# Hybrid convolution and pooling decoder trunk: first gate block of each merge asked for inside the last input block, convolution taps handed out differently in the merge rounds

## The reference, cut to what matters

```python
# per layer, D_MODEL 2048, E = 1024; x (4, 2048, 2048), DEPTH 2
xn   = rms_norm(h, norm_g)
proj = xn @ w_in              # 9 slices of width E, then three gates of width 2048
a_in, a_b, a_c, a_z, b_in, b_z, c_val, c_gate, c_z, gates = split(proj)
y_a = a_b * causal_dwconv(a_c * a_in, 3 taps) * silu(a_z)
y_b = (pooled(b_in) @ pool_w) * pool_scale * silu(b_z)
v   = causal_dwconv(c_val * sigmoid(c_gate), 31 taps) + bias
y_c = silu(layer_norm(v)) * silu(c_z)
up      = [y_a @ w_bo[0], y_b @ w_bo[1], y_c @ w_bo[2]]       # E -> 2048 each
merged  = sum over b of sigmoid(gates[b]) * up[b]
h = h + merged @ w_o
h = h + sigmoid(h @ w_ple_gate) * (p @ w_ple_proj)
```

## Time and profile before

| | us |
|---|---|
| median of 3 runs | 2593.92 (2593.8 to 2594.42) |
| profiled execution | 2592.57 |
| its span, slowest core (core 1) | 2591.0 |
| spans of the eight cores | 2585.6 to 2591.0 |
| busy on core 1: TensorE, VectorE, ScalarE, GpSimd | 2512.6, 1560.5, 556.6, 119.4 |

### The profile page before, as it was taken

One profiled execution on the slowest core, in us unless ns is written; L12 is line 12 of the kernel. 1 busy time (PEld: TensorE's weight loads), 2 busy tenths in 40 slices (PEclk: granted clock), 3 DMA queues, 4 the chain that ended last, 5 costly groups with the idle time before them and its releaser, 6 DMA issues.

```text
span 2591.0 us, 35103 instructions; the slowest of 8 cores (2585.6 to 2591.0 us)
## 1 busy us (share of the span) xinstructions
PE 2512.6 (97%) x15468; PEld 1506.6 (58%) x15468; DVE 1560.5 (60%) x1534; ACT 556.6 (21%) x746; POOL 119.4 (5%) x217
## 2 busy tenths in 40 slices
PE   5999999999999999999999999999999999999997
PEld 2666667776667678766666655544554444444445
DVE  4567666865787753412447676777668885442156
ACT  6000002211212322112340000022112224221124
POOL 0000000000000000000000000000000000000001
PEclk9999999999999999999999999999999999999998
DMA  7434343444344444645553434334434444446453
GB/s 219 88 66 79 69 76 72 82 75 73 73 74 83 92 85 82 143 99 95 132 131 74 75 72 82 73 74 81 86 70 81 91 90 98 83 96 148 84 94 131
DMA packets 49848, 237.51 MB, mean 92 GB/s; under 512 B 4768, under 2 KB 18080, under 8 KB 26912
## 3 DMA queue, kind: packets, MB, share of 16 engines
q0 software_dynamic: 29056, 186.72, 40.1%
q1 hardware_dynamic: 20640, 48.54, 5.6%
HBM read 404.67 MB, written 17.29 MB: 163 GB/s over the span
## 4 chain that ended last, share of the span: by engine, by line
PE 89%; DVE 7%; ACT 1%; SPq 1%; issue 1%; DMA 1%; POOL 0%; DVEq 0%; ACTq 0%; POOLq 0%
PE psa L134 89%; DVE Tt L134 3%; DVE h L134 3%; SPq L134 1%; ACT Tt L134 1%; DVE yb L134 1%; DMA yb<-w_in 1%; DVE acc L134 0%; ACT L134 0%; POOL ring L134 0%; ACT psa L134 0%; ACT yb L134 0%; ACT acc L134 0%; DVEq L131 0%; DVEq L99 0%
## 5 line engine op out<-in xcount | busy, mean ns | idle before, releaser
L134 PE MATMUL psa<-xn,ring 128*128 128x352 bf16 (+8 forms) x8384 | 1365.4, 322 | 9.2 <-DVE Tt L134 5.3
L134 PEld LDWEIGHTS psa<-xn,ring 128*128 128x128 bf16 x8384 | 815.5, 97 | 541.6 <-DVE Tt L134 9.5
L134 DVE SCALAR_TENSOR_TENSOR h<-h,par_s 128x1056 f32<-128x1056 bf16 (+1 forms) x480 | 623.6, 1299 | 11.5
L134 DVE TENSOR_TENSOR Tt<-psa,Tt 128x1056 f32<-128x1056 f32 (+7 forms) x208 | 205.5, 989 | 517.1 <-PE psa L134 477.2
L134 ACT ACTIVATE Tt<-psa 128x512 f32<-128x512 f32 (+9 forms) x328 | 243.2, 742 | 1134.6 <-PE psa L134 1108.2
L134 PE MATMUL psa<-yb,ring 128*128 128x352 bf16 (+1 forms) x1920 | 343.5, 339 | 0.0
L134 PE MATMUL psa<-acc,ring 128*128 128x352 bf16 (+2 forms) x1664 | 292.7, 336 | 31.1 <-DVE acc L134 23.6
L134 PEld LDWEIGHTS psa<-yb,ring 128*128 128x128 bf16 x1920 | 186.5, 97 | 152.2
L134 PEld LDWEIGHTS psa<-acc,ring 128*128 128x128 bf16 x1664 | 161.9, 98 | 159.9 <-DVE acc L134 26.1
L134 DVE TENSOR_TENSOR Tt<-Tt 128x1056 f32<-128x1056 f32 (+9 forms) x130 | 136.0, 1046 | 121.3 <-ACT Tt L134 118.3
L134 PE MATMUL psa<-h 128*128 128x264 bf16 (+1 forms) x1152 | 185.1, 319 | 17.6 <-DVE h L134 16.0
(11 more groups left out here) (70 smaller groups left out, 928.9 us busy)
## 6 DMA issues: line engine op xcount, KB each, us to landing
ring<-w_in POOLq DMA_DIRECT2D x118, 1024.0 KB, 9.0
ring<-w_branch_out POOLq DMA_DIRECT2D x24, 1024.0 KB, 9.0
ring<-w_o POOLq DMA_DIRECT2D x16, 1024.0 KB, 9.6
ring<-w_ple_gate POOLq DMA_DIRECT2D x14, 1024.0 KB, 11.0
h<-xT SPq DMA_DIRECT2D x12, 724.0 KB, 15.7
h<-xT SPq DMA_DIRECT2D x16, 543.0 KB, 8.9
h_keep<-h SPq DMA_DIRECT2D x16, 543.0 KB, 8.8
h<-h_keep SPq DMA_DIRECT2D x16, 543.0 KB, 8.5
```

The source lines that it names most:

```text
L134: ins = getattr(eng, o.meth)(**o.kw)
```

## The change

- `load_gate(b, 0)` moves out of `merge_branch` into the last input block (`j == 3`) of each stage, right behind the load of that block's last weights. In stages A and C this is the same place in the POOL queue as before; in stage B the gate's load now stands ahead of the load of `pool_w` into `side`.
- `weight_sums` of that block moves from the head of the merge to between the groups `i == 0` and `i == 1` of the last input block. In stage A it stands behind the `yb` product of `i == 0` and ahead of its `bg(3)`; in stage B behind the silu of `i == 0`, where `bg(3)` becomes `bg(1)`; in stage C behind `cz_norm` of tile 6 and ahead of that of tile 7.
- In a merge round `bg(4)` becomes `bg(1)`, and the four `bg(1)` behind the `jj` groups become `bg` of 1, 0, 0, 6. The sum stays 14 per round. By the count through the program, 5 taps are left at the head of stage C in place of 3.
- `block_group` gets its rows and temporaries as parameters; with the values given it makes the same instructions.

```diff
-            def merge_branch(b):
-                def load_gate(i):
-                    return load_main(wl[36 + b * 8 + i], 16)
-
+            def load_gate(b, i):
+                return load_main(wl[36 + b * 8 + i], 16)
+
+            def merge_branch(b, slot):
                 pend = deque()
-                slot = load_gate(0)
-                weight_sums(slot)
                 for q in range(4):
-                    nxt = load_gate(2 * q + 1)
-                    block_group(slot, (0, 1), 0, pend)
+                    nxt = load_gate(b, 2 * q + 1)
+                    block_group(slot, (TF(0), TF(1)), 0, pend, u3=TF(4))
                     weight_sums(nxt)
                     bg(6)
                     slot = nxt
                     bo = load_main512(w_bo[l, b, q])
-                    block_group(slot, (2, 3), 0 if nb == 2 else 4, pend)
-                    bg(4)
+                    block_group(slot, (TF(2), TF(3)), 0 if nb == 2 else 4, pend, u3=TF(5))
+                    bg(1)
...
                         if jj == 1 and q < 3:
                             weight_sums(slot)
-                        bg(1)
+                        bg((1, 0, 0, 6)[jj])
...
                 slot = load_main(wl[(3 * E + u[0] * 128) // 256], 16)
+                if j == 3:
+                    gate_slot = load_gate(0, 0)
                 for i in range(2):
...
                     TT(yb[:, u[i], LO:TL], co[:, LO:TL], sz[:, LO:TL], ALU.mult, r_co + r_sz, [r_yb[u[i]]])
+                    if j == 3 and i == 0:
+                        weight_sums(gate_slot)
                     bg(3)
-            merge_branch(0)
+            merge_branch(0, gate_slot)
...
                 slot = load_main(wl[(5 * E + u[0] * 128) // 256], 16)
+                if j == 3:
+                    gate_slot = load_gate(1, 0)
                 for i in range(2):
                     g = mm_group(proj_steps(slot, i * 128, xn, r_xn), R_out)
                     ACT(v3(U[i][0], R_out), pv(g, R_out), AF.Silu, g.res, U[i][1])
-                    bg(3)
+                    if j == 3 and i == 0:
+                        weight_sums(gate_slot)
+                        bg(1)
+                    else:
+                        bg(3)
                 ss = load_side(pool_w[l, j])
...
                 cz_slot[j] = load_main(wl[(8 * E + 2 * j * 128) // 256], 16)
+                if j == 3:
+                    gate_slot = load_gate(2, 0)
                 for i in range(2):
                     cz_norm(*cz_proj(j, i))
+                    if j == 3 and i == 0:
+                        weight_sums(gate_slot)
             reload(range(10, 16))
-            merge_branch(2)
+            merge_branch(2, gate_slot)
```

More of the change, by code:

```diff
@@ L592, in weight_sums, with block_group @@
                 TT(sb[:, 2], q(0, 1), sb[:, 1], ALU.subtract, [rr, r_S[1]], [r_S[2]])
-            def block_group(slot, rows, base, pend):
+            def block_group(slot, rows, base, pend, func=AF.Sigmoid, m5=None, u3=None):
                 b0, b4, b1, b2 = (base + i * nb for i in range(4))
@@ L598, in bank, with tiled @@
                     return psa[:, b:b + nb, 0:N], r_bank[b:b + nb]
+                def tiled(ap):
+                    return ap.rearrange("p (j n) -> p j n", n=N)
                 def half(row, hf):
-                    ap, res = TF(row)
-                    return ap[:, LO + hf * H:LO + hf * H + H].rearrange("p (j n) -> p j n", n=N), [res[hf]]
+                    ap, res = row
+                    return tiled(ap[:, LO + hf * H:LO + hf * H + H]), [res[hf % len(res)]]
                 def prod(b, lhs, rhs, start):
@@ L632, in block_group @@
                 p4, q4 = bank(b4)
-                ua, r_u = TF(4 + rows[0] // 2)
-                u3 = ua[:, 0:H].rearrange("p (j n) -> p j n", n=N)
+                ua, r_u = u3
+                u3 = tiled(ua[:, 0:H])
                 g00, r00 = half(rows[0], 0)
@@ L638, in block_group @@
                 g11, r11 = half(rows[1], 1)
+                if m5 is None:
+                    m5v, r_m = g11, r11
+                else:
+                    m5v, r_m = tiled(m5[0][:, 0:H]), m5[1]
                 prod(b0, wq(0, 0), xh(0, 0), True)
@@ L641, in block_group @@
                 prod(b4, ws(0), xt(0), True)
-                ACT(g11, p4, AF.Copy, q4, r11)
+                ACT(m5v, p4, AF.Copy, q4, r_m)
                 prod(b1, ws(1), xt(1), False)
@@ L647, in block_group @@
                 prod(b0, wq(0, 1), xh(1, 0), False)
-                ACT(g00, p0, AF.Sigmoid, q0, r00)
+                ACT(g00, p0, func, q0, r00)
                 prod(b2, wq(1, 0, r_S3[slot]), xt(2), False)
@@ L651, in block_group @@
                 prod(b1, ws(2), xh(1, 1), False)
-                TT(g01, p1, g11, ALU.add, q1 + r11, r01)
-                TT(g11, u3, g11, ALU.add, r_u + r11, r11)
+                TT(g01, p1, m5v, ALU.add, q1 + r_m, r01)
+                TT(g11, u3, m5v, ALU.add, r_u + r_m, r11)
                 prod(b2, wq(1, 1), xt(3), False)
-                ACT(g10, p2, AF.Sigmoid, q2, r10)
-                pend.append(lambda: ACT(g01, g01, AF.Sigmoid, r01, r01))
-                pend.append(lambda: ACT(g11, g11, AF.Sigmoid, r11, r11))
-            def merge_branch(b):
-                def load_gate(i):
-                    return load_main(wl[36 + b * 8 + i], 16)
+                ACT(g10, p2, func, q2, r10)
+                pend.append(lambda: ACT(g01, g01, func, r01, r01))
+                pend.append(lambda: ACT(g11, g11, func, r11, r11))
+            def load_gate(b, i):
+                return load_main(wl[36 + b * 8 + i], 16)
+            def merge_branch(b, slot):
                 pend = deque()
-                slot = load_gate(0)
-                weight_sums(slot)
                 for q in range(4):
-                    nxt = load_gate(2 * q + 1)
-                    block_group(slot, (0, 1), 0, pend)
+                    nxt = load_gate(b, 2 * q + 1)
+                    block_group(slot, (TF(0), TF(1)), 0, pend, u3=TF(4))
                     weight_sums(nxt)
@@ L672, in merge_branch @@
                     bo = load_main512(w_bo[l, b, q])
-                    block_group(slot, (2, 3), 0 if nb == 2 else 4, pend)
-                    bg(4)
+                    block_group(slot, (TF(2), TF(3)), 0 if nb == 2 else 4, pend, u3=TF(5))
+                    bg(1)
                     if q < 3:
-                        slot = load_gate(2 * q + 2)
+                        slot = load_gate(b, 2 * q + 2)
                     elif b == 2:
@@ L695, in merge_branch @@
                             weight_sums(slot)
-                        bg(1)
+                        bg((1, 0, 0, 6)[jj])
                 state["pg"] = 0
+            zbase = 0 if nb == 2 else 4
             def conv_tap(i, k):
@@ L808, in build_program @@
                         g.res + [r_par] + U[o][1], [r_yb[u[o]]])
-            merge_branch(1)
+            merge_branch(1, gate_slot)
             def cz_proj(jj, i):
```

## The result

The changed kernel takes 2563.86 us (median), 30.1 us less than the 2593.92 of the kernel before beside it. The ratio is 0.988, with a 95% interval of 0.985 to 0.991 (the quotient of the two medians is 0.9884); in a second comparison on another occasion 0.9886 (0.9871 to 0.9902). The profiled execution took 2563.63 us with a span of 2562.1 on its slowest core, core 1 again. The forecast was 2567.7: the sign, the places and the waits were right, but two prices were too low, and the gain was about 4 us larger than the sum.

What follows compares the result with a forecast made beforehand. TensorE, busy 2512.6 of 2591.0 us, bounds the kernel, so only its removed idle time and clock losses count. Gains of 6.68 + 7.67 + 0.75 + 3.84 + 0.57 + 6.87 - 0.2 = 26.2 us give 2567.7; range 2563.5 to 2575.

Steps and rivals of the forecast that it cites:

- Stages A: Start of merge A: sums one group earlier remove wait and clock loss, gaining 6.68 us in layer 0, 7.67 in layer 1.
- Stages B: Start of merge B: gain 0.75 us in layer 1, none in layer 0 (0 to 0.3); `side` still lands in time.
- Stages C: Start of merge C: gain 3.84 us in layer 0, 0.57 (to 2.1) in layer 1, where a 2.15 us wait stays.
- I leave the loss of 1.56 in: Merge C, layer 1: clock loss of 1.56 us assumed to stay behind the remaining wait; gain 0.57 (0.57 to 2.1).
- Turns of rounds: Merge B of layer 0: three turns lose their stall of 2.29 us each, gain 6.87 us.
- Head of stage C: Last convolution tile: eleven taps in place of four cost 0 to 1.4 us in each layer; 0.2 taken in all.
- best case: Whole kernel: every TensorE wait and clock loss goes, gain 30.4 us, time 2563.5 us.
- rival 1: Rounds of merge B keep their stall because the freed banks are still late: 2574.6 us, chance 0.10.
- rival 2: Clock losses do not go with the waits, some fall elsewhere or stay: 5.9 us less gain, 2573.6 us, chance 0.07.
- rival 3: At the moved sums the gate's weights have not landed and VectorE stands; only the rounds gain: 2587.0 us, chance 0.03.
- rival 4: Burst of six taps delays the second block's weight sum in 16 rounds: slower, 2599.7 us at 3 us, chance 0.03.

Runs made afterwards that it cites:

- sums-alone kernel: Changed kernel's early first gate load and four weight sums, with taps handed out as in the kernel before: 2572.86 us, ratio 0.9917 against the kernel before.
- burst of eight: Changed kernel with a round's taps given as 0 behind the second gate block and 0, 0, 0, 8 behind the groups: 2586.77 us.
- sums one tile earlier: Changed kernel with the four sums of merge C ahead of the layer norm of tile 6 in place of behind it: 2564.67 us.
- burst of ten: Changed kernel with 4 taps behind the first block's sums, 0 behind the second gate block and 0, 0, 0, 10 behind the groups: 2636.64 us.

## Why the prediction was right, and where it was off

- **Stages A: right.** The cover of 2.02 us on VectorE, the late `yb` product that nobody waits for, and the clock as part of the price all came as worked out. The sums-alone kernel shows that the place needs nothing else from the change.
- **Stages B: right.** No cost from the swap on POOL; the start in layer 0 gained 0.22, within its bound.
- **Stages C: the mechanism right, the size off.** The wait that remains, its length, its new place before product 3 and its cause (a copy that ScalarE keeps behind the last silu) are shown by two kernels: an earlier place in the chain changes nothing, the pauses of the chain take it away. This agrees with the order of queues that the Trainium skill gives (TensorE: Matmul & The Clock Gate, Architectural detail): the copy starts at 2156.02, behind the silu of 2154.87. The step that failed is "I leave the loss of 1.56 in". With the wait still 2.17 us long the loss came on none of the eight cores of the changed kernel, on one in the sums-alone kernel, and on all eight in the burst of eight. That term was mis-sized by 1.54 us, half of the miss of 3.1 us on core 1. The prediction gave it a bound of 2.1 and took the other end; why the loss stayed away in this kernel is open.
- **Turns of rounds: the mechanism right, the size off by 1.03 us.** The walk along VectorE gave the slack at each step to 0.3 us. What failed is the price of the stall, read off as 1.76 + 0.53 us. Between the same matmuls it is 2.63 us a turn. The bracket counts from the modelled end of the last matmul, and in an unbroken stream the next one starts before that end: product 1 at 397.09 covers 1.97 us, and product 2 starts at 398.90, 0.16 us before its end. The start of merge B in layer 1 shows the same on a single wait: bracket 0.75, gain 0.92. Nine waits that went altogether (the starts of merges A, that of merge B in layer 1, and two at each of three turns) at 0.17 make 1.5 us. In merges C a wait stays and is short by the same, so there it cancels.
- **Head of stage C: right.** The backlog is gone, and the eleven taps end at 859.14, 0.1 us late. It costs 0.08 and 0.33 us, not 1.4 each.
- **The range.** Its low end was the sum with every loss of clock gone, but with brackets as prices. Waits of TensorE are to be taken 0.17 us longer; with that the sum is 27.7, and the best case, in which all eleven waits go, 32.3.
- **The rivals.** The stall in the turns went (rival 1), the four losses went with their waits on core 1 (rival 2), the weights had landed (rival 3), and six taps are a burst that the second block covers (rival 4).

## What to carry to other kernels

Where TensorE is busy 97% of the time, walk the few places where it waits, one engine at a time, to the next thing that will be late: in stage C that was a copy on another engine behind a silu, and the walk gave its wait to 0.02 us before the kernel was built. Work moved into a serial chain of two engines cost its full length at both places of the chain that were tried; put it into the pauses in which one engine waits for the other. Background work belongs behind the instruction that frees a buffer, in a burst no longer than the cover up to the next one that somebody waits for, and that limit can be worked out and tested from both sides.

## What the runs showed of the hardware that was not expected

- A wait of one and the same length may cost TensorE its clock or not. Behind 2.15 to 2.17 us before product 3 in layer 1: no core of eight in the changed kernel, one of eight with the sums alone and one with the sums one tile earlier, all eight with the burst of eight (3.40 to 3.58 us for 8 matmuls, against 1.90), none with the burst of ten. Behind 2.29 us: five of eight. Behind 3.83 us: all eight. In the kernel before, the five cores that lose behind the 2.38 us in layer 0 (0, 1, 4, 6 and 7) are the five that lose behind the 2.72 us in layer 1. On core 7 of the burst of ten three waits of 2.35 us, at the three turns of merge A in layer 0, are followed by a loss, none, and a loss (5.44, 3.77 and 5.44 us). What decides isn't settled by these runs.
- Shorter waits can be followed by a loss too. In the merges no loss was seen behind waits of up to 1.76 us, but at the end of the changed kernel two waits of 0.67 and 1.17 us with one short matmul between them are followed by a loss on three of eight cores (2, 3 and 4). Core 3, then core 1, timeline of TensorE:

```profile
2532.96 0.28 PE L134 MATMUL psa<-yb,ones_s 128*128 128x256 bf16 x1 [0.67 <-ACT yb L134]
2534.41 0.28 PE L134 MATMUL psa<-yb,ones_s 128*128 128x256 bf16 x1 [1.17 <-ACT yb L134]
2534.53 3.50 PE L134 MATMUL psa<-xn,ring 128*128 128x256 bf16 x16
```

```profile
2534.66 0.28 PE L134 MATMUL psa<-yb,ones_s 128*128 128x256 bf16 x1 [1.18 <-ACT yb L134]
2534.78 1.91 PE L134 MATMUL psa<-xn,ring 128*128 128x256 bf16 x16
```

- Gains at separate places add up to 0.01 us between kernels with the same list of matmuls, where no loss of clock is in between; the places at which they don't are those behind a wait of over 2 us.
- The bracket before a matmul that waited is about 0.17 us shorter than what the wait costs.
